# Router to experts: gathered rows copied in one go, a conversion ahead of the token copies, the shared product ahead of the choice of experts

## What is computed

```python
s = jax.nn.sigmoid((xf @ router_w).astype(jnp.float32))
sb = s + router_b.astype(jnp.float32)
gscore = jnp.sum(lax.top_k(sb.reshape(-1, N_GROUPS, EXPERTS_PER_GROUP), TOP_K)[0], axis=-1)
gsel = jnp.argmax(gscore, axis=-1)                       # one group of 4 experts
_, idx = lax.top_k(jnp.where(emask, sb, -jnp.inf), TOP_K)  # two experts in it
wsel = jnp.take_along_axis(s, idx, axis=-1)
gate = ...                                               # wsel over its sum, per expert
out = _swiglu(xf, sg, su, sd)                            # the shared expert
out = out + gate[:, e:e + 1] * _swiglu(xf, wg[e], wu[e], wd[e])   # for 16 experts
```

## Time and profile before

| what | us |
|---|---|
| median of 3 runs | 997.51 (997.17 to 997.89) |
| the profiled execution | 998.19 |
| its span, first to last instruction | 996.3 |
| TensorE, VectorE, ScalarE busy | 959.4, 823.3, 673.0 |
| stretch from the router to expert 0, layer 0 | about 327 to 341.6 |
| same stretch, layer 1 | about 817 to 832 |

### The profile page before, as it was taken

The page is one execution under the profiler, slowest core; times in us unless marked ns, Lnnn a source line. Parts: engine busy times, 40 slices in busy tenths (PEclk is TensorE's granted clock), DMA queues, the critical chain, the costliest instruction groups (busy, mean ns, idle before and its releaser), DMA issues.

```text
span 996.3 us, 24157 instructions
## 1 busy us (share of the span) xinstructions
PE 959.4 (96%) x9862; PEld 748.8 (75%) x9862; DVE 823.3 (83%) x1484; ACT 673.0 (68%) x1092; POOL 0.7 (0%) x10
## 2 busy tenths in 40 slices
PE   9999999999999899999999999999999989999994
PEld 7877777777776799965578777777777768999652
DVE  6796767776789899998888876678768889999986
ACT  7665555866365899886677545568653659998764
POOL 0000000000000000000000000000000000000000
PEclk9999999999999999999999999999999999999998
DMA  9855444323564299998736544443344425999951
GB/s 366 335 170 160 136 152 129 130 86 128 169 221 141 87 368 379 379 364 299 265 108 233 175 121 142 154 130 95 119 146 151 155 79 177 384 374 397 367 208 56
DMA packets 59651, 205.01 MB, mean 206 GB/s; under 512 B 7216, under 2 KB 10348, under 8 KB 59020
## 3 DMA queue, kind: packets, MB, share of 16 engines
q1 hardware_dynamic: 56748, 198.08, 57.1%
q10 hardware_dynamic: 2784, 5.28, 1.6%
HBM read 198.76 MB, written 3.40 MB: 203 GB/s over the span
## 4 chain that ended last, share of the span: by engine, by line
PE 65%; DVE 18%; ACT 8%; issue 5%; DVEq 2%; DMA 1%; ACTq 0%; SPq 0%
PE bank L1880 42%; DVE wlo L1135 9%; PE bank L1904 4%; ACT whi L593 4%; PE bank L2425 3%; DVE xT L1148 2%; PE bank L1909 1%; PE bank L2242 1%; DVE xlo L1154 1%; PE bank L2441 1%; PE bank L1949 1%; DVEq L1186 1%; PE bank L2174 1%; DVE mu_var L1187 1%; PE bank L2345 1%
## 5 line engine op out<-in xcount | busy, mean ns | idle before, releaser
L1135 DVE SCALAR_TENSOR_TENSOR wlo<-w,whi 128x1024 f16<-128x1024 f32 x358 | 428.1, 1217 | 61.5 <-ACT whi L593 60.2
L593 ACT ACTIVATE whi<-w 128x1024 f16<-128x1024 f32 x358 | 370.0, 1050 | 79.2 <-PE bank L1880 52.9
L1880 PE MATMUL bank<-xhi,whi 128*128 128x320 f16 x688 | 206.1, 300 | 0.8 <-DVE wlo L1135 0.8
L1880 PE MATMUL bank<-xhi,wlo 128*128 128x320 f16 x688 | 205.7, 299 | 0.0
L1880 PE MATMUL bank<-xlo,whi 128*128 128x320 f16 x688 | 205.7, 299 | 0.0
L1880 PE MATMUL bank<-arena_b,whi 128*128 128x112 f16 x2048 | 159.4, 213 | 3.4 <-DVE wlo L1135 3.2
L1880 PE MATMUL bank<-arena_b,wlo 128*128 128x112 f16 x1024 | 156.0, 213 | 0.0
L1880 PEld LDWEIGHTS bank<-arena_b,whi 128*128 128x128 f16 x2048 | 149.8, 98 | 5.3 <-issue 3.1
L1880 PEld LDWEIGHTS bank<-arena_b,wlo 128*128 128x128 f16 x1024 | 100.2, 98 | 0.4 <-issue 0.4
L1880 PEld LDWEIGHTS bank<-xhi,whi 128*128 128x128 f16 x688 | 67.2, 98 | 28.5 <-DVE wlo L1135 1.1
L1880 PEld LDWEIGHTS bank<-xhi,wlo 128*128 128x128 f16 x688 | 67.3, 98 | 26.2
(11 more groups left out here) (377 smaller groups left out, 1755.2 us busy)
## 6 DMA issues: line engine op xcount, KB each, us to landing
w<-in_w SPq DMA_DIRECT2D x358, 512.0 KB, 5.0
arena_b<-head_rows ACTq DMA_DIRECT2D x2, 1920.0 KB, 9.8
rows<-in_rows SPq DMA_DIRECT2D x2, 1024.0 KB, 10.0
xT<-in_x SPq DMA_DIRECT2D x2, 640.0 KB, 5.5
out_y<-xT SPq DMA_DIRECT2D x4, 320.0 KB
out_ckv<-arena_a SPq DMA_DIRECT2D x2, 320.0 KB
acc<-kr SPq DMA_DIRECT2D x2, 288.0 KB
arena_c<-kr SPq DMA_DIRECT2D x2, 288.0 KB
```

Source lines behind the costliest of these rows:

```text
L593: A(whi[:, n % SLOTS, :], w32[:, n % RAW, :], ACT.Copy, scale=WS).then_inc(hi_done.sem, 1)
L1135: V.scalar_tensor_tensor(wlo[:, n % SLOTS, :], w32[:, n % RAW, :], WS, whi[:, n % SLOTS, :], ALU.mult, ALU.subtract).then_inc(lo_done.sem, 1)
L1880: ins = M(out, w[:, s, sub * P:(sub + 1) * P], rhs(part, k), start=(n == 0), stop=(n == 3 * len(subs) - 1))
```

## The change

ScalarE takes the conversion of U0+5 ahead of the token copies, writes the four gathered copies behind each other, and moves `hi` of U0+6 behind them and the gates' high half behind `hi` of U0+7. VectorE takes the first shared product and `lo` of U0+5 ahead of the choice of two experts; the functions only move with it, unchanged. TensorE's slotting of the gates moves from behind block 0 to behind block 1 of expert 0, and the gate rows of expert 0 from behind block 2 to behind block 3.

```diff
@@ ScalarE
                 shared_tanh(0)
                 hi_lead(U0 + 1)
+                hi_lead(U0 + 2)
                 for j in range(4):
                     x_tokens(j)
-                hi_lead(U0 + 2)
...
                     for q in range(4):
-                        if q == 2:
-                            hi_lead(U0 + 3)
-                            gates_hi()
                         act.wait_ge(xg_ps.sem, xg_ps.value(l, q + 1))
                         A(x_grp[:, 0, q // 2, 4 * (q % 2):4 * (q % 2) + 4, :], bank[5 + q % 2][:, 0:4 * CAP]
                           .rearrange("p (k n) -> p k n", k=4), ACT.Copy).then_inc(xg_ev.sem, 1)
+                    hi_lead(U0 + 3)
                     act.wait_ge(u_free.sem, u_free.value(l, 1))
                     shared_tanh(1)
                     shared_hi(0)
                     hi_lead(U0 + 4)
+                    gates_hi()
                     act.preload_act_table_set(SILU)
@@ VectorE
                 V.tensor_copy(most_i[:, :], most[:, :]).then_inc(most_set.sem, 1)
+                def hidden_product(n, ready1, f, W, gate):
...
+                def hidden_lo(n, W, c0, gate):
...
+                hidden_product(0, U0 + 2, 0, T, None)
+                lo_lead(U0 + 2)
                 for n, o in enumerate((O1, O2)):
...
-                hidden_product(0, U0 + 2, 0, T, None)
                 dve.wait_ge(most_set.sem, most_set.value(l, 1))
                 dve.wait_ge(gt_h.sem, gt_h.value(l, 1))
                 V.scalar_tensor_tensor(gt_lo[:, :, :], rt[:, 7], GS, gt_hi[:, :, :], ALU.mult,
                                        ALU.subtract).then_inc(gt_l.sem, 1)
-                lo_lead(U0 + 2)
                 lo_lead(U0 + 3)
@@ TensorE
-                                        if e == 0 and j == 0:
+                                        if e == 0 and j == 1:
                                             gate_slots()
-                                        if j == (0 if e else 2):
+                                        if j == (0 if e else 3):
                                             pe.wait_ge(g_lo.sem, g_lo.value(l, 1))
```

More of the change, by code:

```diff
@@ L1681, in _ @@
                 V.tensor_copy(most_i[:, :], most[:, :]).then_inc(most_set.sem, 1)
+                def hidden_product(n, ready1, f, W, gate):
+                    dve.wait_ge(u_tanh.sem, u_tanh.value(l, n + 1))
+                    V.scalar_tensor_tensor(h1[:, 0:W], ht[:, 0:W], 1.0, bank[UPB[2 * f]][:, 0:W], ALU.add,
+                                           ALU.mult)
+                    dve.drain()
+                    dve.wait_ge(blk_done.sem, blk_done.value(l, ready1))
+                    V.tensor_tensor(h1[:, 0:W], h1[:, 0:W], bank[UPB[2 * f + 1]][:, 0:W], ALU.mult
+                                    ).then_inc(u_free.sem, 1)
+                    dve.drain()
+                    if gate is not None:
+                        dve.wait_ge(gb_ps.sem, gb_ps.value(l, gate))
+                        V.tensor_tensor(h2[:, 0:W], h1[:, 0:W], bank[4][:, 0:W], ALU.mult
+                                        ).then_inc(u_prod.sem, 1)
+                    else:
+                        V.tensor_copy(h2[:, 0:W], h1[:, 0:W]).then_inc(u_prod.sem, 1)
+                def hidden_lo(n, W, c0, gate):
+                    dve.wait_ge(u_hi.sem, u_hi.value(l, n + 1))
+                    scale = UN * UN * XS / (2 if gate is None else 2 * GS)
+                    V.scalar_tensor_tensor(hlo[:, bass.ds(c0, W)], h2[:, 0:W], scale,
+                                           hhi[:, bass.ds(c0, W)], ALU.mult, ALU.subtract
+                                           ).then_inc(u_lo.sem, 1)
+                hidden_product(0, U0 + 2, 0, T, None)
+                lo_lead(U0 + 2)
                 for n, o in enumerate((O1, O2)):
```

## The result

The changed kernel takes 999.81 us (median of 11 runs, 999.26 to 1000.68), the kernel before 997.51 in the same session (11 runs, 997.03 to 998.03). The ratio is 1.0024 with a 95% interval of 1.0015 to 1.0034: slower, by 2.3 us. The forecast was 999.7. The profiled execution of the changed kernel took 999.99, its span is 998.1.

The account below looks back on a forecast made before the run. The prediction took VectorE as the real limit just behind the router, with 0.26 and 0.19 us of slack at block U0+9. Lateness of 1.07 + 1.14 = 2.2 us on the 997.51 median gave 999.7, forecast range 999.4 to 1000.6.

Parts of the forecast that it names:

- (b): Four gathered copies on ScalarE: with 0.36 us branch delay the last ends at 340.31, so expert 0 may start 0.83 earlier.
- (d): VectorE at the gates' low half: a new wait from 341.88 to 343.05, making it late by 1.23 us net.
- (a): ScalarE's hi of U0+5 ahead of the token copies: its 0.95 us fits in 1.01 of idle, cost nothing.
- the lower end: No branch delay on ScalarE before the gathered copies: expert 0 may start 0.96 us earlier, total 999.4.
- (c): ScalarE's queue ahead of the gate conversion: it starts at 342.77 and ends at 343.02, where before it ended at 340.27.
- (e): TensorE waits for VectorE's low halves: block U0+9 starts 1.07 us later in layer 0, 1.14 in layer 1.
- (f): The weight transfer of U0+13 is issued 4.6 us earlier; taken as worth zero.
- Rival A: First group of experts: spare time on VectorE and ScalarE takes back half the lateness; +1.1 us, 998.6; chance 0.25.
- Rival B: Gates' low half: the gate conversion ends before 341.95, so the new wait doesn't decide; at best 997.2; chance 0.12.
- Rival C: DMA paces the full stretches: the block fetched early gives 1.40 us a layer against 1.1 lost; 997.0; chance 0.05.
- rival D: Gathered copies: the branch costs more than its bounds, or the gate matmuls wait as well; above 1000.6; chance 0.06.
- My sum of 2.2: TensorE's lateness at block U0+9 over both layers, 1.07 + 1.14 us, added to the median before.

Follow-up runs that it names:

- e4: The kernel before with only ScalarE's hi of U0+5 moved ahead of the token copies; 997.30 us (before 997.51).
- e6: The changed kernel with VectorE's lo of U0+5 and of U0+6 both between the choice of experts and the gates' low half; 998.33 us (before 997.30).
- e1: The changed kernel with VectorE's order of before: shared product and lo of U0+5 back behind the choice of experts; 1004.73 us (before 997.51).
- e3: The changed kernel with VectorE's lo of U0+5 behind the choice of experts, the product still ahead of it; 999.82 us (before 997.51).
- e2: The changed kernel with ScalarE's gate conversion one place earlier, ahead of hi of U0+7; 998.11 us (before 997.51).
- e7: As e6, with the low half of the second shared product moved behind lo of U0+9; 997.84 us (before 997.30).
- e8: As e4, with the low half of the second shared product moved behind lo of U0+9; 997.02 us (before 997.30).
- e10: The changed kernel: gate conversion right behind hi of U0+6, lo of U0+5 as in e3, second product's low half as in e7; 997.26 us (before 997.55).
- e11: As e10, but the shared product behind the choice of experts and lo of U0+5 behind the gates' low half; 998.77 us (before 997.55).
- e9: The kernel before with TensorE's part alone: gate matmuls behind block 1, gate rows behind block 3 of expert 0; 998.43 us (before 997.30).
- e5: The kernel before with VectorE's part alone: first shared product and lo of U0+5 ahead of the choice of experts; 1010.26 us (before 997.55).

## Why the prediction was right

The mechanism is shown, and the time was 0.1 off. That closeness is partly luck: the interval of the difference runs from 1.5 to 3.4 us, and two small errors in the sum, in (b) and (d), cancel.

(a) Right. The token copies start at the same place and their idle is gone; e4, this part alone, is not slower.

(b) The branch: I took 0.36 of delay between 0 and 0.79, the runs show none that counts. In the changed kernel the first gathered copy starts 0.30 after the token copies end, released by TensorE's gather, so the branch's own delay is hidden behind that. This is close to the lower end: the last copy ends at 340.22, where I had 340.31 and the lower end 340.18. Expert 0 then starts 0.99 earlier instead of 0.83, and all of it is lost again at U0+8. The Trainium skill, Advanced Engine Details and Errata, section Control Flow Timing, gives about 108 ns for a compare-and-branch. The branch's own rows on ScalarE have less, 37 to 53 ns, and either is small beside 0.36. The dear part is the value load ahead of the branch, as e6 shows on VectorE; on ScalarE it runs while the last token copies do.

(c) The four steps ahead of the gate conversion: I had it at 342.77, it came at 342.69 on the stretch's clock. This is the branch's error, nothing else. What stands behind it I had within 0.3 of the place before; the copy of the slotted gates came 0.52 later, since TensorE writes them later. In this kernel that cost nothing, as `lo` of U0+8 was later still.

(d) The wait was 1.17 by my count and 1.12 in the trace. The hand-over from ScalarE through a separate wait took 0.10 where I had 0.03, which made up for most of (c). VectorE's net lateness, predicted 1.23, is 1.22 in both layers. That it is not due to VectorE's own reorder is shown by e1 and e3, that it is ScalarE's place for the gate conversion by e2.

(e) Predicted 1.07 and 1.14 at U0+9, measured 1.02 and 1.08. For the hand-over I had 0.10 from no row; it was 0.06 at this block. That TensorE can't take it back is shown by the end of the group, and by the rows of the table: what it has at U0+9 stays until U0+26 to within 0.02, except where it was then earlier than VectorE's low half of U0+12 allows (e7, e8, e10, e11). I took the TensorE part to be free; it is so only in company (e9).

(f) No transfer was waited for; the early one gave nothing.

Rival A is wrong, nothing of the lateness came back. Rival B's condition didn't arise here: the gate conversion ended at 342.93 on the stretch's clock, not before 341.95. The gain that it allows is small, as e4 and e10 show: 0.1 to 0.4 at U0+9, 0.1 to 0.2 a layer at the end. Rival C has no sign, and rival D's costs didn't come: the branch was cheap, and the gate matmuls waited 0.2. My sum of 2.2 stands beside 2.3 by the runs and 2.1 by the profiles without their pauses.

What stays open: the two pauses in the profile of the kernel before, why the clock falls at about 319 us in some executions and not in others, and what the slower executions of e5 lost.

## What to carry to other kernels

When an engine is left with an early start, look for the engine that feeds it next and read its slack, block by block: here VectorE had 0.26 us at U0+9 and 0.39 at U0+12, hand-over included, and a start 0.99 us earlier was worth 0.17 (e10). A small conversion that a second engine waits for belongs ahead of a long one, not behind it: one place in ScalarE's order was worth 1.7 us. A wait is not filled by moving work that was ahead of it already; only work from behind it counts, and of that leave one long instruction to cover a branch. And when TensorE stands idle for some microseconds, count its clock behind the wait as well: in e1 and e5 it cost more than a microsecond a layer.

## What the runs showed that I had not expected

- A value load into a register and a branch cost VectorE 0.50 us of bare time when only a short waiting instruction ran ahead of them, and nothing when a 1.2 us one did (e6 against e10).
- TensorE's granted clock was 0.64 and 0.79 in two stretches of 3 us, in code that the change doesn't touch, and cost 0.45 us. The same came in e9 and e10, and in layer 1 of e2, and in no other profile; TensorE had been busy 1.44 of the 3.00 us before them in both kernels.
- TensorE's clock was halved behind a long wait: granted 0.50 after 2.57 us of idle in e1 and after 5.19 in e5. A lateness of 2.35 us on VectorE became 3.60 in e1, by way of TensorE and ScalarE, and one of 4.16 on TensorE became 5.53 in e5.
